# Inverse square roots of four norms on GpSimd in a two-layer decoder trunk

## The reference

```python
def _rmsnorm(x, g):
    xf = x.astype(jnp.float32)
    y = xf * lax.rsqrt(jnp.mean(xf * xf, axis=-1, keepdims=True) + EPS)
    return (y * g.astype(jnp.float32)).astype(x.dtype)

def reference(x, mem, ...):
    mem_n = _rmsnorm(mem, mem_norm_g)
    for i in range(DEPTH):
        h = _rmsnorm(x, mix_norm_g[i])
        mix = ...   # SSD or stick-breaking, beside attention of h into mem_n
        x = x + mix
        x = x + _swiglu(_rmsnorm(x, ffn_norm_g[i]), ffn_w_gate_up[i], ffn_w_down[i])
    return x

def _memory_attention(q, mem_n, w_kv, q_g, k_g):
    q = _rmsnorm(q.reshape(b, s, MEM_HEADS, MEM_HEAD_DIM), q_g)   # a norm per head
    k, v = jnp.split(mem_n @ w_kv, 2, axis=-1)
    k = _rmsnorm(k.reshape(b, m, MEM_HEADS, MEM_HEAD_DIM), k_g)
    ...
```

## Time and profile before

| | |
|---|---|
| median of three runs | 815.62 us (815.34 to 815.93) |
| the profiled execution | 815.59 us, span 813.5 us |
| PE busy | 804.1 us (99%), granted clock 9 tenths or more in every slice |
| DVE, ACT, POOL busy | 541.8 us (67%), 437.5 us (54%), 62.9 us (8%) |
| L940, DVE subtraction to `lo`, x132 | 296.5 us, mean 2252 ns |
| L627, ACT rounding to `hi`, x132 | 245.6 us, mean 1862 ns |
| L1253 PE `lo` by `aT_hi`, x672 | 264.2 us, mean 393 ns |

### The profile page before, as it was taken

The page is one execution under the profiler, slowest core; times in us unless marked ns, Lnnn a source line. Parts: engine busy times, 40 slices in busy tenths (PEclk is TensorE's granted clock), DMA queues, the critical chain, the costliest instruction groups (busy, mean ns, idle before and its releaser), DMA issues.

```text
span 813.5 us, 9762 instructions
## 1 busy us (share of the span) xinstructions
PE 804.1 (99%) x3858; PEld 672.1 (83%) x3858; DVE 541.8 (67%) x746; ACT 437.5 (54%) x520; POOL 62.9 (8%) x80
## 2 busy tenths in 40 slices
PE   9989999999999999999999999999999999999998
PEld 8977888888888888888888888888888888888886
DVE  6678989997758555455347878578767755555442
ACT  5657775466537444434326576667653744445330
POOL 4000013530000000000000000113220000000000
PEclk9999999999999999999999999999999999999999
DMA  7844466443446656555555545443445556565561
GB/s 242 286 155 157 131 219 213 149 169 105 159 155 205 198 167 204 174 189 191 177 202 171 191 155 158 153 155 105 154 156 155 178 184 200 168 202 171 191 207 52
DMA packets 85292, 141.38 MB, mean 174 GB/s; under 512 B 3406, under 2 KB 50672, under 8 KB 85248
## 3 DMA queue, kind: packets, MB, share of 16 engines
q1 hardware_dynamic: 84256, 139.60, 52.3%
q10 hardware_dynamic: 608, 1.06, 0.3%
q0 software_dynamic: 384, 0.11, 0.1%
HBM read 139.68 MB, written 1.07 MB: 173 GB/s over the span
## 4 chain that ended last, share of the span: by engine, by line
PE 80%; DVE 12%; ACT 3%; issue 2%; DMA 1%; SPq 0%; DVEq 0%; ACTq 0%
PE acc L1253 24%; PE acc L1255 24%; PE acc L1254 24%; PE bank L1250 4%; DVE lo L940 4%; DVE zs L1053 2%; DMA raw<-in_ssd_w_in 1%; ACT hi L627 1%; DVE seg L1073 1%; DVE seg L1081 1%; PE bank L1447 1%; PE bank L1425 1%; DVE hg L1073 1%; ACT sq L627 1%; ACT zs L627 1%
## 5 line engine op out<-in xcount | busy, mean ns | idle before, releaser
L940 DVE TENSOR_TENSOR lo<-raw,hi 128x2048 fp32r<-128x2048 f32 (+2 forms) x132 | 296.5, 2252 | 130.8 <-ACT hi L627 130.6
L627 ACT ACTIVATE hi<-raw 128x2048 fp32r<-128x2048 f32 (+2 forms) x132 | 245.6, 1862 | 72.1 <-DMA raw<-in_ffn_w_down 47.3
L1253 PE MATMUL acc<-lo,aT_hi 128*128 128x512 f32 (+1 forms) x672 | 264.2, 393 | 1.3 <-DVE lo L940 0.9
L1255 PE MATMUL acc<-hi,aT_lo 128*128 128x512 f32 (+1 forms) x672 | 258.9, 385 | 0.0
L1254 PE MATMUL acc<-hi,aT_hi 128*128 128x512 f32 (+1 forms) x672 | 258.4, 385 | 0.0
L1253 PEld LDWEIGHTS acc<-lo,aT_hi 128*128 128x128 f32 x672 | 126.3, 188 | 25.6 <-issue 1.1
L1255 PEld LDWEIGHTS acc<-hi,aT_lo 128*128 128x128 f32 x672 | 126.1, 188 | 25.7
L1254 PEld LDWEIGHTS acc<-hi,aT_hi 128*128 128x128 f32 x672 | 126.4, 188 | 23.8
L1253 PE MATMUL acc<-lo,uT_hi 128*128 128x512 f32 x176 | 68.7, 391 | 0.0
L1255 PE MATMUL acc<-hi,uT_lo 128*128 128x512 f32 x176 | 68.5, 389 | 0.0
L1254 PE MATMUL acc<-hi,uT_hi 128*128 128x512 f32 x176 | 68.5, 389 | 0.0
(11 more groups left out here) (200 smaller groups left out, 869.2 us busy)
## 6 DMA issues: line engine op xcount, KB each, us to landing
raw<-in_ffn_w_gate_up SPq DMA_DIRECT2D x88, 512.0 KB, 4.8
raw<-in_ffn_w_down SPq DMA_DIRECT2D x22, 1024.0 KB, 4.9
raw<-in_sb_w_in SPq DMA_DIRECT2D x20, 1024.0 KB, 5.0
raw<-in_ssd_w_in SPq DMA_DIRECT2D x14, 1024.0 KB, 5.1
raw<-in_mem_w_kv SPq DMA_DIRECT2D x8, 1024.0 KB, 5.0
raw<-in_ssd_w_out SPq DMA_DIRECT2D x8, 1024.0 KB, 4.9
raw<-in_sb_w_out SPq DMA_DIRECT2D x8, 1024.0 KB, 4.9
seg<-cs_rows SPq DMA_DIRECT2D x6, 384.0 KB, 4.7
```

The costliest lines, as they stand in the source:

```text
L627: return nc.scalar.activation(out_, in_, func, **k)
L940: v.tensor_tensor(lo[w % RING][:, c], raw[w % RING][:, c], hi[w % RING][:, c].bitcast(F), ALU.subtract).then_inc(lo_ready, 1)
L1253: mm(ps, stat_hi, mov_lo, start=first, stop=False)
L1255: return mm(ps, stat_lo, mov_hi, start=False, stop=last)
```

## The change

`POOL_NORMS` names the head norms of qm0 and km0. For these `hn` is replaced by two steps: `hs`, in which DVE sums the squares and POOL computes the inverse square root, and `hm`, one unit later, in which DVE multiplies. Both stand in `MIDDLE`, behind the subtraction of their unit. The transposes of qm0 go from unit 7 to unit 8, so that `memT` comes before them and takes the earlier banks. The row norm of x and that of memory are computed on POOL, the latter in unit 9 in place of 12. POOL's `rsqrt` has 14 instructions: it halves in the Newton step instead of once ahead, and has no fused operation. The other eight head norms and the row norms 1 to 3 stay as they are.

```diff
--- before.py
+++ after.py
@@ -87,6 +87,7 @@
 GC = [(g, c) for g in range(GROUPS) for c in range(TOK)]
 
 
+POOL_NORMS = ["qm0", "km0"]
 HEAD_NORMS = ["qm0", "km0", "km1", "qm1", "k0", "k1", "k2", "q0", "q1", "q2"]
 
 
@@ -111,9 +112,9 @@
     at(1, ("par", 1))
     at(4, ("dt",))
     at(6, ("cs",))
-    at(7, ("hT", "qm0", 0), ("hT", "qm0", 1))
+    at(8, ("hT", "qm0", 0), ("hT", "qm0", 1))
     at(8, ("memsq",))
-    at(12, ("memnorm",))
+    at(9, ("memnorm",))
     at(8, ("csT",))
 
     for i, u in enumerate((2, 8, 10, 12, 14)):
@@ -187,7 +188,12 @@
     k = block_end("qm1") + 4
     memory_attention(1, (k, k + 2, k + 2, k + 4), (k + 5, k + 5, k + 8, k + 8), (k + 6, k + 12))
     for n in HEAD_NORMS:
-        at(block_end("dtq1" if n == "qm0" else n) + 1, ("hn", n))
+        e = block_end("dtq1" if n == "qm0" else n)
+        if n in POOL_NORMS:
+            at(e + 1, ("hs", n))
+            at(e + 2, ("hm", n))
+        else:
+            at(e + 1, ("hn", n))
     input_transposes(U_FFN1 - 1, 3)
 
 
@@ -195,9 +201,9 @@
 
 
 
-NO_BANK = ("gate", "silu", "seg", "segm", "pn", "dt", "memsq", "memnorm", "sps", "zd", "hn")
-
-EARLY, MIDDLE = ("seg", "pn", "zd", "sps", "hn"), ("segm",)
+NO_BANK = ("gate", "silu", "seg", "segm", "pn", "dt", "memsq", "memnorm", "sps", "zd", "hn", "hs", "hm")
+
+EARLY, MIDDLE = ("seg", "pn", "zd", "sps", "hn"), ("segm", "hs", "hm")
 USES = {s: i for i, s in enumerate(s for u in sorted(PLAN) for s in PLAN[u] if s[0] not in NO_BANK)}
 
 NAT = {"B": ("xb", 0, 1), "qm0": ("hT", "qm0", 1), "C": ("xb", 1, 1), "xs0": ("xb", 2, 1),
@@ -262,6 +268,7 @@
         da, cs, ecs, dte = cols(2 * HEADS), cols(2 * HEADS), cols(HEADS), cols(HEADS)
         ssq_x, rstd_x = cols(2), [cols(2) for _ in range(5)]
         ssq8, r8, v8, h8, t8 = cols(8), cols(8), cols(8), cols(8), cols(8)
+        pv8, pt8 = cols(8), cols(8)
         ssqy, ry = cols(8), cols(8)
         mx, sums, rsum = cols(4), cols(8), cols(2)
         gq_scaled = cols(1)
@@ -591,6 +598,41 @@
                 yg = y[:, c, g * GW:(g + 1) * GW].rearrange("p (h n) -> p h n", n=HP)
                 nc.gpsimd.tensor_tensor(yg, yg, each(d_b[:, heads_of(0, g)], HP), ALU.mult).then_inc(S("skip"), 1)
 
+            made = [0]
+
+            def link(ins):
+                made[0] += 1
+                ins.then_inc(S("pool_seq"), 1)
+                pool.wait_ge(S("pool_seq"), made[0])
+
+            def rsqrt(dst, ssq, n, count, done):
+
+                g = nc.gpsimd
+                a, t = pv8[:, 0:n], pt8[:, 0:n]
+                link(g.tensor_scalar(a, ssq, 1.0 / count, EPS, ALU.mult, ALU.add))
+                link(g.tensor_scalar(dst.bitcast(I32), a.bitcast(I32), -0.5, float(0x5f3759df), ALU.mult, ALU.add))
+                for i in range(3):
+                    link(g.tensor_tensor(t, dst, dst, ALU.mult))
+                    link(g.tensor_tensor(t, t, a, ALU.mult))
+                    link(g.tensor_scalar(t, t, -0.5, 1.5, ALU.mult, ALU.add))
+                    last = g.tensor_tensor(dst, dst, t, ALU.mult)
+                    if i < 2:
+                        link(last)
+                last.then_inc(done, 1)
+
+            def row_norm(p, i):
+                pool.wait_ge(S("x_ssq"), TOK * i)
+                if i > 1:
+                    pool.wait_ge(S("rstd"), i - 1)
+                rsqrt(rstd_x[p], ssq_x, 2, D, S("rstd"))
+
+            def head_rsqrt(name):
+                pool.wait_ge(S("head_ssq"), POOL_NORMS.index(name) + 1)
+                pool.wait_ge(S("rstd"), 1)
+                rsqrt(r8, ssq8, 8, P, S("head_rstd"))
+
+            row_norm(0, 1)
+
             def diag_mask(v):
                 return nc.gpsimd.tensor_tensor(v, v, whole(tlt[:], 2), ALU.mult)
 
@@ -599,6 +641,10 @@
                     kind = step[0]
                     if kind == "seg":
                         scan_inputs(step[1], step[2])
+                    elif kind == "hs":
+                        head_rsqrt(step[1])
+                    elif kind == "memnorm":
+                        row_norm(4, 2)
                     elif kind == "yo":
                         g = step[1]
                         wait_read(pool, ("yd", g, 1))
@@ -749,7 +795,8 @@
                     dt_scan()
                 elif kind == "memsq":
                     act.wait_ge(S("mem_landed"), 32)
-                    act.wait_ge(S("nat_normed"), 1)
+                    act.wait_ge(S("head_ssq"), 1)
+                    act.wait_ge(S("rstd"), 1)
                     sum_squares(4, memn)
                 elif kind == "cs":
                     wait_read(act, step)
@@ -1023,8 +1070,6 @@
                     link(v.tensor_scalar(gq_scaled, vcol[:, SQ_:SQ_ + 1], SCALE, None, ALU.mult))
                 elif kind == "memT" and step[2] == 0:
                     input_tile(step)
-                elif kind == "memnorm":
-                    row_norm(4, 2)
                 elif kind == "dt":
                     dve.wait_ge(S("head_vectors_landed"), 48)
                     for t in range(TOK):
@@ -1171,6 +1216,12 @@
                                                ALU.subtract))
                 elif kind == "hn":
                     head_norm(step[1])
+                elif kind == "hs":
+                    dve.wait_ge(S("squares"), HEAD_NORMS.index(step[1]) + 1)
+                    v.reduce_sum(ssq8, sq[:].rearrange("p (h n) -> p h n", n=P), axis=AX.X).then_inc(S("head_ssq"), 1)
+                elif kind == "hm":
+                    dve.wait_ge(S("head_rstd"), HEAD_NORMS.index(step[1]) + 1)
+                    head_scale(step[1])
                 elif kind == "sps":
                     dve.wait_ge(S("sp_hi"), step[1] // 2 + 1)
                     v.tensor_tensor(sp_parts[1][:], spb[:], sp_parts[0][:].bitcast(F),
@@ -1186,6 +1237,9 @@
                 dve.wait_ge(S("squares"), i + 1)
                 link(v.reduce_sum(ssq8, sq[:].rearrange("p (h n) -> p h n", n=P), axis=AX.X))
                 rsqrt(r8, ssq8, 8, P, S("head_rstd"), i + 1)
+                head_scale(name)
+
+            def head_scale(name):
                 b = natb(name)[:].rearrange("p t (h n) -> p (t h) n", n=P)
                 v.tensor_tensor(b, b, each(r8, P), ALU.mult).then_inc(S("nat_normed"), 1)
 
@@ -1193,7 +1247,6 @@
                 if u == -1:
                     steps(("par", 0))
                     first_inputs()
-                    row_norm(0, 1)
                     continue
                 if u in ENDS and ENDS[u][0] == "rows":
                     i = ENDS[u][2] + 1
```

## The result

The changed kernel takes **819.02 us** in the median of six runs (818.81 to 820.88), the one before 815.58: ratio 1.0046 (95% interval 1.0033 to 1.0059), slower by 3.4 us. Forecast were 816.4, with a range to 818.6.

What follows compares the result with a forecast made beforehand. PE, busy 99% of the span, was taken to bound the kernel, so only its idle time could be won. Sum: -4.9 + 1.45 + 1.0 + 3.3 = +0.85 us on 815.59, 816.4 us; range 812.8 to 818.6.

Steps and rivals of the forecast that it cites:

- Point 1: Row norm of x, at the start: POOL's chain is shut out by a `lo`, and PE loses 1.0 us.
- The price of an instruction: One tiny POOL instruction that waits for the one before it, in the new `rsqrt`: taken as 0.245 us.
- R: Time of POOL's 14-instruction inverse square root: 3.4 us against 2.6 on DVE, bounds 2.3 and 4.5.
- Point 2: Head norm of qm0, its transposes one unit later: 2.9 us of PE stops becomes 1.1.
- Point 3: Row norm of memory off DVE: stops for `lo` and `xsn` go; PE leaves unit 15 some 2.45 us earlier.
- T: PE's end of unit 15, from which the times at km0 are counted; 104.45 us before the change.
- The blocking: A POOL instruction that meets a DVE subtraction of two SBUF tiles waits for its whole end, 2.2 us per `lo`.
- Rival A: POOL's tiny instructions are not caught by DVE subtractions (812.9 us), or R is near 2.3 (814.0 us); chance 0.25.
- rival C: Unseen load or first-use cost of POOL at 20 us; 5 us in its place would give 821; chance 0.03.
- Point 4: Head norm of km0: scaling ends at T + 16.2, PE waits from T + 12.9, 3.3 us; bounds 2.2 and 4.4.
- B: Wait for km0's head norm outgrows the early units' gain: at R = 4.5, +3.4, 819.0 us; chance 0.25.

Runs made afterwards that it cites:

- the run with the scaling first: Changed kernel, but DVE scales km0 ahead of the low part of unit 17, not behind it: 815.38 us, ratio 0.9997 to the kernel before.
- the matmuls of constants: Changed kernel with 14 constant matmuls on PE ahead of the wait for km0's norm, filling the stop: 817.17 us; with 28, 820.22 us.

## Why the prediction was wrong

**Point 1, x: right.** One hole of 1.29 us (forecast 1.2), eviction from 24.72 (24.6), PE idle 1.2 before `xb` (0.9). PE started at 26.13 where the sum had 25.85: half of that is the price of an instruction, and 0.15 lies between the end of ACT's evictions (24.72 + 1.26 = 25.98) and PE's start, which the sum left out.

**The price of an instruction: too low.** 0.28 us against my 0.245, R = 3.86 on 8 columns against 3.4. I had 0.16 for its own length and 0.08 for the gap behind it; they are 0.20 and 0.08. R lies inside the bounds, 2.3 and 4.5, and the rows of before did not set it closer.

**Point 2, qm0: right.** Scaling from 52.37 (52.0), stops 0.8 and 0.3 for the memory tiles (0.7 and 0.4), those at 47 us gone. The pair stands in the waits.

**Point 3, memory: right in kind.** Its chain was not held, though I had listed a gap under a `lo` for each of the four. The stops for `lo` and `xsn` went, that for `G` (0.3) stayed. ACT's eviction of km0, 0.03 behind T, came at 102.56 in place of 104.48: 1.92 us won where I had 2.45. Of the 0.5, 0.2 is x's longer stop. The stops for the memory tiles are as long as I had them, 1.1 together, but I had counted a restart of 0.16 for each stop that went and none for these two.

**The blocking: right, and decisive.** Rival A fell: the small instructions waited for whole subtractions, and the run with the scaling first took the wait away with the subtraction. The same run speaks against rival C, a first-use cost, as do 0.18 and 0.19 us for POOL's first two TENSOR_SCALAR at 19.82 and 20.08.

**Point 4, km0: the step that failed.** Its wait was there, 3.7 us idle, and 3.86 counted as in the prediction (T = 102.53, + 12.94 = 115.47, to 119.33); I had 3.3, and most of the excess is R. But the prediction put the stop down at its length: "PE waits from T + 12.9: 3.3 us", and the sum ends with it. What was left out is what a stop of this length does to PE's clock. The stops that the earlier trace rows show had been 1.7 us at most, and the clock stayed full through them, so no row of before priced a longer one; I named the clock only among the signs that would make the forecast wrong. The runs price it: 1.85 us by the matmuls of constants, 1.65 by the timeline. The Trainium skill (TensorE: Matmul & The Clock Gate, "What's actually happening") describes such a gate, full rate when busy and half when idle, and in "Why this matters for your kernels" advises against long idle gaps between bursts of matmuls. The trace agrees, with 0.50 granted behind 3.7 us of idleness. I had not weighed this rule against my own stop.

With the terms as measured: -1.92 at T, +3.86 at km0, +1.65 of clock, 3.6 against 3.44. Without the clock 815.6 - 1.92 + 3.86 = 817.5; the filled stop gave 817.17. So of the 2.6 us between forecast and time some 0.8 to 1.1 is R and the smaller gain ahead of km0, and 1.65 to 1.85 the clock, without which the time would have been inside the range.

**The rivals.** B was right in part. Its condition, R from 3.8 on, was met with 3.86, and the wait for km0 did outgrow what the early units gained, 3.86 against 1.92. But by R alone that makes 817.2 to 817.5. B reached the right time, 819.0, only with R = 4.5; what was missing at R = 3.86 was the clock, so that its number agrees is luck. The range, which ended at 818.6, left B's own time out. A forecast that had carried 1.65 of clock on its own 3.3 us would have been near 818, if a stop of 3.3 lowers the clock too, which no run here shows.

## What to carry to other kernels

A dependent chain of tiny instructions moved to GpSimd isn't dearer by its own speed alone: each instruction that reads SBUF can wait out a whole VectorE subtraction of two SBUF tiles, so it belongs where VectorE has a pause or runs from PSUM (as beside the chain of memory here), and only where the consumer has that much slack (qm0 had it behind a unit, km0 had 2.5 us). When a new stop of TensorE comes out as several microseconds, price the granted clock behind it as well, and see first whether another order keeps the stop short: against the same kernel without it, a stop of 1.7 us cost 1.6 (815.38 against 813.77) and one of 3.7 cost 5.3 (819.02). Time an edit's parts by themselves before judging the whole.

## What the runs showed of the hardware

A GpSimd TENSOR_SCALAR or TENSOR_TENSOR on 128 x 2 or 128 x 8 float32 took 0.18 to 0.20 us, and some 0.28 from start to start where each waits for the last; on VectorE the like was 0.17 and 0.20. One on 8 columns was held for 2.17 and 2.27 us by a 128 x 2048 subtraction of two SBUF tiles; those on 2 columns beside a convolution that reads a PSUM bank kept their 0.19. After the same idle time of 3.7 us the granted clock was low for 3.4 us in one kernel and for 6.8 us in another (119.9 to 126.8), in which it fell before PE had restarted; what sets the difference was not tried. After a stop of 1.7 us it stayed at 1.00. A matmul of 128 columns in plain float32 took PE 0.23 us, as long as one of 512 columns on the rounded parts (fp32r); a float32 transpose of 128 took 0.11.
